# Down projection of the prompt tokens in seven products of half blocks instead of eight, with its sums made by GpSimd through DRAM

## What is computed

```python
D_MODEL, D_FF = 1024, 2816      # 1024 prompt tokens, 64 sample tokens, fp32

def _swiglu(x, w_gate, w_up, w_down):
    return (jax.nn.silu(x @ w_gate) * (x @ w_up)) @ w_down

x = _layernorm(ALPHA * x + 0.5 * _swiglu(x, ffa_w_gate, ffa_w_up, ffa_w_down), ln1_g, ln1_b)
x = _layernorm(ALPHA * x + m, ln2_g, ln2_b)          # m: the token mixer
x = _layernorm(ALPHA * x + 0.5 * _swiglu(x, ffb_w_gate, ffb_w_up, ffb_w_down), ln3_g, ln3_b)
```

## Time and profile before

| | |
|---|---|
| median of the runs | 2540.74 us |
| span of the profiled execution, first to last instruction | 2539.2 us |
| TensorE (PE) busy | 2455.0 us, 97% |
| VectorE (DVE) busy | 1393.8 us, 55% |
| ScalarE (ACT) busy | 962.4 us, 38% |
| GpSimd (POOL) busy | 266.7 us, 11% |
| up stage of block a, down stage of block a | 457.25 us and 270.62 us on the chain |

### The profile page before, as it was taken

The page is one execution under the profiler, slowest core; times in us unless marked ns, Lnnn a source line. Parts: engine busy times, 40 slices in busy tenths (PEclk is TensorE's granted clock), DMA queues, the critical chain, the costliest instruction groups (busy, mean ns, idle before and its releaser), DMA issues.

```text
span 2539.2 us, 52563 instructions
## 1 busy us (share of the span) xinstructions
PE 2455.0 (97%) x21526; PEld 2158.9 (85%) x21526; DVE 1393.8 (55%) x2536; ACT 962.4 (38%) x1682; POOL 266.7 (11%) x309
## 2 busy tenths in 40 slices
PE   7999999999999999999999999998999999999997
PEld 7999999988777788766657988876899999998776
DVE  6555555645335747767633445554756565664623
ACT  5333333434214747534323333433433333343411
POOL 3000000000003211000000122334200000000102
PEclk9999999999999999999999999999999999999999
DMA  4222222555416444422113021245122222274431
GB/s 137 85 69 86 68 86 85 170 192 175 137 37 191 119 124 119 134 60 65 33 46 123 29 68 65 82 170 177 56 86 68 86 72 82 92 238 156 143 136 39
DMA packets 263291, 265.81 MB, mean 105 GB/s; under 512 B 35697, under 2 KB 199618, under 8 KB 261522
## 3 DMA queue, kind: packets, MB, share of 16 engines
q1 hardware_dynamic: 218738, 223.40, 27.8%
q10 hardware_dynamic: 43104, 36.31, 4.4%
q0 software_dynamic: 1216, 2.80, 0.4%
HBM read 203.88 MB, written 58.04 MB: 103 GB/s over the span
## 4 chain that ended last, share of the span: by engine, by line
PE 89%; DVE 3%; ACT 3%; issue 2%; DMA 1%; POOL 1%; SPq 0%; ACTq 0%; POOLq 0%; DVEq 0%
PE ps_b L522 18%; PE ps_a L522 18%; PE ps_a L532 11%; PE ps_b L532 11%; PE ps_rk L2697 6%; PE ps_pj L1170 4%; PE ps_wo L3492 4%; PE ps_mp L1885 2%; PE ps_mp L1911 2%; PE ps_pj L1152 1%; PE ps_mp L1899 1%; PE ps_rk L2787 1%; PE ps_mp L1870 1%; PE ps_rk L2693 1%; PE ps_rk L2839 1%
## 5 line engine op out<-in xcount | busy, mean ns | idle before, releaser
L522 PE MATMUL ps_b<-X_b,W_b 128*128 128x272 f32 x3696 | 464.8, 289 | 4.3 <-DVE X_b L722 4.3
L522 PEld LDWEIGHTS ps_b<-X_b,W_b 128*128 128x128 f32 x3696 | 464.6, 189 | 4.5 <-DVE X_b L722 4.5
L522 PE MATMUL ps_a<-X_a,W_a 128*128 128x272 f32 x3696 | 463.8, 288 | 3.3 <-DVE X_a L722 2.3
L522 PEld LDWEIGHTS ps_a<-X_a,W_a 128*128 128x128 f32 x3696 | 463.2, 189 | 3.9 <-DVE X_a L722 2.5
L532 PE MATMUL ps_a<-W_a,X_a 128*128 128x512 f32 (+1 forms) x1188 | 270.8, 390 | 0.0
L532 PE MATMUL ps_b<-W_b,X_b 128*128 128x512 f32 (+1 forms) x1188 | 270.8, 390 | 0.0
L532 PEld LDWEIGHTS ps_a<-W_a,X_a 128*128 128x128 f32 (+1 forms) x1188 | 215.9, 182 | 54.5
L532 PEld LDWEIGHTS ps_b<-W_b,X_b 128*128 128x128 f32 (+1 forms) x1188 | 215.9, 182 | 54.5
L587 ACT ACTIVATE W_a<-wraw_a 128x512 fp32r<-128x512 f32 x154 | 96.4, 627 | 224.6 <-PE ps_a L532 125.2
L587 ACT ACTIVATE W_b<-wraw_b 128x512 fp32r<-128x512 f32 x154 | 96.4, 627 | 220.6 <-PE ps_b L532 125.1
L763 DVE TENSOR_TENSOR W_b<-wraw_b,W_b 128x512 fp32r<-128x512 f32 x154 | 110.0, 715 | 114.4 <-ACT W_b L587 114.1
(11 more groups left out here) (441 smaller groups left out, 3859.1 us busy)
## 6 DMA issues: line engine op xcount, KB each, us to landing
wraw_a<-in_ffa_w_down SPq DMA_DIRECT2D x44, 512.0 KB, 4.0
wraw_b<-in_ffb_w_down SPq DMA_DIRECT2D x44, 512.0 KB, 4.0
wraw_pj<-in_w_in SPq DMA_DIRECT2D x28, 512.0 KB, 4.0
wraw_a<-in_ffa_w_gate SPq DMA_DIRECT2D x22, 512.0 KB, 4.7
wraw_a<-in_ffa_w_up SPq DMA_DIRECT2D x22, 512.0 KB, 4.8
hidden<-G_a ACTq DMA_DIRECT2D x22, 512.0 KB, 3.1
wraw_b<-in_ffb_w_gate SPq DMA_DIRECT2D x22, 512.0 KB, 4.8
wraw_b<-in_ffb_w_up SPq DMA_DIRECT2D x22, 512.0 KB, 4.7
```

What stands on the lines that cost most here:

```text
L522: last = nc.tensor.matmul(ps[:, bank + p, :PIECE], W[:, n % WC, wp, k * P:(k + 1) * P], operand(i, xp)[:, k, p * PIECE:(p + 1) * PIECE], s ...
```

## The change

The down projection of the 1024 prompt tokens is cut into half blocks: tokens (tiles 0 to 3, tiles 4 to 7), hidden dimension (11 blocks, 11 blocks) and output (512, 512 columns). Seven products of half blocks replace eight. Their operands are sums: four sums of quarters of the down weights and four of quarters of the gated activation. GpSimd makes both during the up stage: in `differences(e)` it takes blocks of down weights that SyncE has loaded for it, and SyncE stores the results in DRAM; in `hidden_sums(e)` it adds the four quarters of the gated activation, and ScalarE issues the stores (`send_sums`). The sample tokens don't take part: their high and low parts lie side by side as one operand of 128 columns, which goes by the high and the low part of the weights (two passes), and `token_low` and `token_sum` fold the halves.

Its core:

```diff
+            def differences(e):
+                pool.wait_ge(Q.d_in.h, Q.d_in.at(32 * (e + 1)))
+                for k, (out, a, b) in enumerate(((0, 1, 0), (1, 3, 1), (3, 3, 0), (2, 2, 3))):
+                    if k >= 1:
+                        pool.wait_ge(Q.d_made.h, Q.d_made.at(4 * e + k))
+                    G_.tensor_tensor(hraw[:, out, :512], hraw[:, a, :512], hraw[:, b, :512], ALU.subtract).then_inc(Q.d_made.h, 1)
+
+            def hidden_sums(e):
+                if e >= 1:
+                    pool.wait_ge(Q.hs_out.h, Q.hs_out.at(48 * e))
+                q = [SG[:, j, :512] for j in range(4)]
+                pool.wait_ge(Q.h_made.h, Q.h_made.at(4 * e + 4))
+                G_.tensor_tensor(s1, q[1], q[3], ALU.add).then_inc(Q.hs_made.h, 1)
+                pool.wait_ge(Q.hs_made.h, Q.hs_made.at(4 * e + 1))
+                G_.tensor_tensor(s2, s1, q[0], ALU.subtract).then_inc(Q.hs_made.h, 1)
+                G_.tensor_tensor(q[1], q[0], q[1], ALU.subtract).then_inc(Q.hs_made.h, 1)
+                pool.wait_ge(Q.hs_made.h, Q.hs_made.at(4 * e + 2))
+                G_.tensor_tensor(s4, q[2], s2, ALU.subtract).then_inc(Q.hs_made.h, 1)
...
+            for u in range(UNITS):
+                if u >= 2 and u % 2 == 0:
+                    hidden_sums(u // 2 - 1)
+                if u < NE:
+                    differences(u)
+            hidden_sums(NE - 1)
```

SyncE, in the up stage:

```diff
             for l in range(4, 2 * UNITS):
                 load_w(l)
+                e, g = divmod(l - 6, 2)
+                if 1 <= e <= NE and g == 0:
+                    store_difference(e - 1)
+                if 0 <= e < NE and g == 1:
+                    load_difference(e)
```

ScalarE, in the up stage and at its end:

```diff
             def silu(e, j):
                 u = 2 * e
                 if j == 0:
                     act.wait_ge(Q.slot_done.h, Q.slot_done.at(7 * u + 3))
                     if e >= 1:
-                        act.wait_ge(Q.h_out.h, Q.h_out.at(64 * e))
-                    nc.scalar.activation(halves(SG[:, 0, :]), bank_pair(0), ACT.Silu).then_inc(Q.silu_made.h, 1)
+                        act.wait_ge(Q.h_out.h, Q.h_out.at(48 * e))
+                        act.wait_ge(Q.hs_made.h, Q.hs_made.at(4 * e))
+                    nc.scalar.activation(halves(SG[:, 0, :]), pair_bank(0), ACT.Silu).then_inc(Q.silu_made.h, 1)
...
+            def send_sums(e):
+                act.wait_ge(Q.hs_made.h, Q.hs_made.at(4 * e + 4))
+                act.dma_start(h_dram[1:5:3, e].rearrange("i p c -> p i c"), Z[:].rearrange("p (i c) -> p i c", i=2)).then_inc(Q.hs_out.h, 16)
+                act.dma_start(h_dram[5, e], SG[:, 1, :512]).then_inc(Q.hs_out.h, 16)
+                act.dma_start(h_dram[3, e], s4).then_inc(Q.hs_out.h, 16)
...
-                    if i == 1 and g == 0 and e >= 1:
+                    if i == 0 and g == 0 and e >= 1:
                         send_hidden(e - 1)
+                    if i == 2 and g == 0 and e >= 1:
+                        send_sums(e - 1)
                     if g == 0 and i == 2:
                         silu(e, 0)
...
+            token_hi(0)
+            h_hi(6)
+            h_hi(7)
             send_hidden(NE - 1)
+            send_sums(NE - 1)
```

TensorE, in the down stage; `i` is the product, `j` the block of the hidden half, `a` the tile:

```diff
+            def down_part(i, j, a):
+                n, s = weights_of(i, j), NE * i + j
                 for m, (hp, wp) in enumerate(((0, 0), (0, 1), (1, 0))):
+                    last = nc.tensor.matmul(ps[:, banks_of(i)[a], :], hidden(s, hp)[:, a * P:(a + 1) * P], W[:, n % WC, wp, :],
+                                            start=(i != 2 and j == 0 and m == 0), stop=(j == NE - 1 and m == 2), skip_group_check=True)
...
+            def token_part(i, j):
+                if j == 0:
+                    if i == 0:
+                        pe.wait_ge(Q.tok_lo.h, Q.tok_lo.at(1))
...
+                for a in range(2 if i == 0 else 1):
+                    bank = SET_B[2 + a] if i == 0 else banks_of(i + 1)[0]
+                    for wp in range(2):
+                        last = nc.tensor.matmul(ps[:, bank, :], tok[:, f, :], W[:, (weights_of(i, j) + a) % WC, wp, :],
...
+            def down_slot(i, j):
+                pe.wait_ge(Q.w_split.h, Q.w_split.at(weights_of(i, j) + (2 if i == 0 else 1)))
+                pe.wait_ge(Q.hlo_made.h, Q.hlo_made.at(NE * i + j + 1))
+                tokens = i in (0, 2, 3)
```

More of the change, by code:

```diff
@@ L216, in __init__ @@
         self.w_in = [sem(f"w_in{u}") for u in range(WB)]
-        self.h_in = [sem(f"h_in{u}") for u in range(HR)]
+        self.h_in = [sem(f"h_in{u}") for u in range(HR // 2)]
         self.stored = [sem(f"stored{u}") for u in range(XS)]
@@ new lines, in load_tokens, with load_difference @@
+            def load_tokens(part):
+                e = slice(0, NE - 1) if part == 0 else slice(NE - 1, NE)
+                sp.wait_ge(Q.h_out.h, Q.h_out.at(48 * (NE - 1 + part)))
+                if part == 0:
+                    wait_weight_slot(sp, UP - 5)
+                out = tok_raw[:].rearrange("p (e g) c -> p e (g c)", g=2)[:, e, :]
+                sp.dma_start(out, tok_dram[e].rearrange("e p c -> p e c")).then_inc(Q.tok_in.h, 16)
+            def load_difference(e):
+                if e == 0:
+                    sp.wait_ge(Q.slo_made.h, Q.slo_made.at(4 * 5))
+                else:
+                    sp.wait_ge(Q.d_out.h, Q.d_out.at(16 * e))
+                for g in range(2):
+                    sp.dma_start(hraw[:, 2 * g:2 * g + 2, :512], down[:, :, e + g * NE, :]).then_inc(Q.d_in.h, 16)
@@ L471, in _ @@
                 for u in range(XS):
-                    sp.wait_ge(Q.stored[u].h, Q.stored[u].at(16 * len(range(u, NT, XS))))
+                    sp.wait_ge(Q.stored[u].h, Q.stored[u].at(16 * sum(stored_by(t) == u for t in range(NT))))
         @blk.tensor
@@ new lines, in h_hi, with token_hi @@
+            def h_hi(s):
+                u, whole = s % HR // 2, min(s | 1, DSLOTS - 1)
+                act.wait_ge(Q.h_in[u].h, Q.h_in[u].at(16 * sum(v % HR // 2 == u for v in range(whole + 1))))
+                if s >= HC:
+                    act.wait_ge(Q.product_done.h, Q.product_done.at(s - HC + 1))
+                else:
+                    wait_weight_slot(act, UP - 7 + s // 4)
+                copy(hidden(s, 0), hidden_raw(s)).then_inc(Q.hhi_made.h, 1)
+            def token_hi(part):
+                f = tokens_of(part)
+                act.wait_ge(Q.tok_in.h, Q.tok_in.at(16 * (part + 1)))
+                if part == 0:
+                    wait_weight_slot(act, UP - 5)
+                copy(tok[:, f, :TS], tok_raw[:, f, :]).then_inc(Q.tok_hi.h, 1)
@@ L890, in _ @@
+            for p in range(5, NT):
+                half_stats(p, 1)
+            for a in range(4):
+                p = 5 + a
+                take("c21", a)
+                half_stats(p, 0)
+                variance(p)
+                if a >= 1:
+                    left(p - 1)
+                inverse(p)
             left(NT - 1)
```

656 lines of the change are left out of this document (412 added, 244 removed).

## The result

The changed kernel takes **2629.95 us** (2626.2 to 2631.77, four runs) against 2543.11 us before (2537.37 to 2550.41, four runs). The ratio is 1.0342, with a 95% interval of 1.0325 to 1.0359. The forecast was 2523 us, so it missed size and sign. The span of the profiled execution is 2629.6 us, 90.4 more than before.

The account below looks back on a forecast made before the run. The prediction took TensorE to bound the kernel, with 89% of the chain. Its terms, -80.2 + 50 + 12 + 1 = -17 us on a span of 2539.2, gave 2522, and 2523 us for the runs' median; range 2485 to 2550.

Parts of the forecast that it names:

- The count: Down stage: 1012 matmuls at 0.228 us in place of 1188, 40.1 us less for each block, 80.2 us for both.
- The last two rivals: Down stage starves on DMA (2600 us), or the count brings less than its share (a few us); starved or other 0.10.
- When the weights for the differences are there: Up stage: the load for GpSimd's differences follows the unit's pair of weight loads and lands at +2.4 us of the even unit.
- The chain from the data to the snapshot: Even up units: GpSimd's eight operations take 14 us, snapshot at +20.1 against +15.1; TensorE stands 5.0 us, ten times, +50 us.
- The term for alternation: Up stage: five two-input VectorE operations come between GpSimd's eight at the shared port, 5 x 0.6 us of the 14 us.
- The odd units, and those from 12 on: Up stage: no snapshot waits in odd units, no differences from unit 12 on; 0, at most 1 us for each odd unit.
- The turn: From up to down: the first token part waits for `token_lo` behind VectorE's queue and GpSimd's sums; 5.9 us, twice, +12 us.
- The product boundaries: Down stage: two token parts want a bank emptied inside 2.73 us; 0.3 us for each, 1 us in all.
- The tail: End of the down stage: tile by tile as before, GpSimd's adds done 15 us before they are wanted; 0 (-1 to +2 us).
- the wait outgrows the gain: Rival, up stage: last sum at +20 or later, loads late beside stores or alternation; 9.5 us a unit, 2571 us, chance 0.13.

Follow-up runs that it names:

- e2: Against the changed kernel: SyncE stores a block's differences right behind their load, ahead of the next pair of weight loads; 2576.6 us.
- e4: Against the changed kernel: the split of the sample tokens' activation moves from behind the last up slot to behind slot 5 of the last up unit; 2612.3 us.
- e7: Against the changed kernel: sums before differences, tokens split early, GpSimd's last additions held back until VectorE's last split, and layernorm of four rows earlier; 2488.67 us.
- e9: Against e7: GpSimd's last eight additions in tile order, VectorE's statistics of the second halves spread between the tiles of the end; 2482.13 us.

## Why the prediction was wrong, by its steps

- **The count** (-80.2): right, -81.4 without waits. The rate of 0.228 us and the price of the token passes held, and no matmul of the down stage waited for DMA, at 308 GB/s from 604 to 640 us and 170 GB/s from 706 to 777. The last two rivals fall.
- **When the weights for the differences are there: the step that failed.** The prediction has them at +2.4 us of the even unit; they came at +11.9. It let SyncE issue the load of the differences together with the unit's pair of weight loads and the store right behind it. The description above says that `load_w` waits for the weights five loads back. That is a misreading: `WB` is 4 (the 5 in that line is `XS`). With five, an odd and the next even load would form the pair; with four it is an even and its odd load. The earlier trace rows already showed it: both loads of the pair come from `in_ffa_w_up`, so they belong to one unit. In the order of SyncE the store of the differences before stands between these two, so it goes only when the next pair of weight loads may go, and the next load of differences waits for it to land. In unit 4 of block a the pair begins at -3.2, the load goes 7.0 us later, and its data come 8.0 us after that (7.4 to 8.6 in the other four): +11.9.
- **The chain from the data to the snapshot** (14 us for GpSimd's eight operations): right in its links, too long in this one. The term for alternation, five VectorE operations between GpSimd's, was mis-sized: the eight took 10.3 us in the changed kernel and 12.1 in e2, because VectorE runs out of work when ScalarE stands. For the changed kernel 9.5 us later and 3.7 us shorter make 5.0 + 5.8 = 10.8 us, measured 10.7. That e2 has 4.97 us, as forecast, is in part luck: its data come 1.4 us late and its operations end 1.9 us sooner after them.
- **The clock: a term that the sum did not have.** Behind the gaps of this kernel, 5.3 to 11.8 us long, the matmuls ran for a while at the lower clock: this cost 22 us in the up stages and 8.5 in the down stages. The prediction priced all its stalls as pure waiting.
- **The odd units, and those from 12 on** (0): right, no gap there.
- **The turn** (+12): right in cause and size: 10.6 us of waiting, and e4, which takes it away, gains 18 with the clock.
- **The product boundaries** (+1): 0.0 us of idle time was recorded at the token parts in e4.
- **The tail** (0, "done 15 us before they are wanted"): wrong. I asked only who waits for the additions and not who is held by them. GpSimd's eight additions and eight layernorm halves held VectorE's last splits back: 11.7 us a block.
- **The rival that came true** is "the wait outgrows the gain", with 9.5 us a unit for 10.0 measured. Its cause is near the measured one but not the same: it has loads that land late beside the stores, and here the load was not issued until a store had landed. It had a chance of 0.13 and 2571 us; the clock (31 us) and the end (23 us) make up most of the other 59. Its line "slower than before from 8 us a unit" doesn't follow from its sum, which breaks even at 6.7; 8 us is where the loss leaves the noise of 13 us.

## What to carry to other kernels

In a queue with a fixed order, the work that someone waits for comes first and the work with slack behind it: swapping the two in GpSimd's order gained 117 us, more than the change had lost. Follow each buffer's round trip (load, use, store, next load) through the constants that set the pairs before pricing it. When work goes to GpSimd beside a busy VectorE, ask also whom it holds, to the last instruction, since each of its operations can cost a waiting VectorE split 1.1 us; and price a gap of TensorE like those of the up stage here (4.5 us in e2, 10.4 us in the changed kernel) at 2 us above its length.

## What was not expected of the hardware

- What a gap costs in clock did not go with its length: five gaps of 5 us in block a left the up stage's busy time at 474.0 us, and so did five of 10.4 us; without them it is 463.8. A gap of 3.7 us was uncertain: behind it L639 was busy for 214.8 us (e7, block b) up to 217.5 (e9, block b), against 214.6 without a gap.
- GpSimd alone does a 128x512 operation in 1.26 us, beside a full VectorE queue in up to 1.75, while a VectorE split goes from 0.69 to 1.78 us. Where both queues are full, an operation moved off VectorE thus still holds VectorE up by 1.1 us, more than the 0.69 us that VectorE would have spent on it.
